# Thirty-two more tokens by gathered rows, one part of the one-hot products on ScalarE, and one block's search in an earlier stage

## The reference, cut to what matters

```
q = (xc @ w_q).reshape(T, 8, 2, 128)
sc = einsum('chpd,hpkd->chpk', q, sub_keys)          # 2 x 128 scores a head
top_s, top_i = top_k(sc, 16)
cand = top_s[:, :, 0, :, None] + top_s[:, :, 1, None, :]
best_s, best_flat = top_k(cand.reshape(T, 8, 256), 16)
expert = ia * 128 + ib                               # 128 experts a token, of 16,384
g = softmax(best_s)
a = gelu(einsum('cd,chkd->chk', xc, u[expert])) * g
out = einsum('chk,chkd->cd', a, v[expert])
```

## Time and profile before

| | |
|---|---|
| median of 3 runs | 1765.27 us (1763.88 to 1772.72) |
| profiled execution, its own time | 1763.86 us |
| its span (first to last instruction) | 1762.0 us, mean granted clock 0.99 |
| PE, PEld, DVE, ACT, POOL busy | 1681.3, 1550.5, 1346.3, 654.0, 401.3 us |
| moved by DMA | 425.82 MB, 242 GB/s over the span |

### The profile page before, as it was taken

One profiled execution on the slowest core, in us unless ns is written; L12 is line 12 of the kernel. 1 busy time (PEld: TensorE's weight loads), 2 busy tenths in 40 slices (PEclk: granted clock), 3 DMA queues, 4 the chain that ended last, 5 costly groups with the idle time before them and its releaser, 6 DMA issues. The chain is left out here.

```text
span 1762.0 us, 26368 instructions
## 1 busy us (share of the span) xinstructions
PE 1681.3 (95%) x9808; PEld 1550.5 (88%) x9808; DVE 1346.3 (76%) x2819; ACT 654.0 (37%) x1027; POOL 401.3 (23%) x282
## 2 busy tenths in 40 slices
PE   5999999999789999999999999999999999999996
PEld 4897766687578999999999999999999999999996
DVE  5433555563566789989989989859988897989898
ACT  5114544441242433443434444433333332333331
POOL 0000000000001021112100112235544554555450
PEclk9999999999899999999999999999999999999998
DMA  5721111022234477778767769999999999999992
GB/s 168 196 89 48 49 48 37 13 86 84 69 93 136 145 276 238 232 251 288 272 252 248 270 213 349 346 385 392 404 366 404 401 396 383 385 390 395 385 402 82
DMA packets 157886, 425.82 MB, mean 242 GB/s; under 512 B 15912, under 2 KB 77520, under 8 KB 155840
## 3 DMA queue, kind: packets, MB, share of 16 engines
q1 hardware_dynamic: 96400, 229.52, 36.8%
q0 software_dynamic: 39472, 144.28, 22.3%
q10 hardware_dynamic: 21888, 50.34, 7.7%
HBM read 365.87 MB, written 58.21 MB: 241 GB/s over the span
## 5 line engine op out<-in xcount | busy, mean ns | idle before, releaser
L431 PE MATMUL psS<-hT_lo,hi 128*128 128x384 f32 (+2 forms) x1504 | 526.6, 350 | 6.6 <-DVE hT_lo L953 5.9
L432 PE MATMUL psS<-hT_hi,lo 128*128 128x384 f32 (+2 forms) x1504 | 518.1, 344 | 0.0
L433 PE MATMUL psS<-hT_hi,hi 128*128 128x384 f32 (+2 forms) x1504 | 515.6, 343 | 0.0
L422 DVE TENSOR_TENSOR lo<-raw,hi 128x1024 fp32r<-128x1024 f32 x323 | 395.0, 1223 | 107.6 <-ACT hi L418 106.2
L418 ACT ACTIVATE hi<-raw 128x1024 fp32r<-128x1024 f32 x323 | 339.0, 1050 | 148.2 <-PE psS L433 111.1
L431 PEld LDWEIGHTS psS<-hT_lo,hi 128*128 128x128 f32 x1504 | 283.5, 188 | 34.8 <-issue 14.8
L541 POOL DMA_INDIRECT gat<-in_u_rows,idx x128 | 185.6, 1450 | 536.0 <-DVE gat L1099 488.4
L433 PEld LDWEIGHTS psS<-hT_hi,hi 128*128 128x128 f32 x1504 | 284.7, 189 | 13.2
L432 PEld LDWEIGHTS psS<-hT_hi,lo 128*128 128x128 f32 x1504 | 284.2, 189 | 10.8
L541 POOL DMA_INDIRECT gat<-in_v_exp,idx x128 | 199.1, 1555 | 197.2 <-DVE y_row L1105 156.5
L708 ACT ACTIVATE act_hi<-act_t 128x384 fp32r<-128x384 f32 x128 | 67.3, 526 | 340.0 <-DVE act_t L1146 340.0
(11 more groups left out here) (278 smaller groups left out, 2540.0 us busy)
## 6 DMA issues: line engine op xcount, KB each, us to landing
raw<-in_u_exp SPq DMA_DIRECT2D x128, 512.0 KB, 4.2
raw<-in_v_exp SPq DMA_DIRECT2D x128, 512.0 KB, 11.3
gelu_dram<-gelu ACTq DMA_DIRECT2D x128, 192.0 KB, 4.0
gel_in<-gelu_dram SPq DMA_DIRECT2D x128, 192.0 KB, 12.1
gates_dram<-gates ACTq DMA_DIRECT2D x12, 1792.0 KB, 9.6
raw<-in_w_merge SPq DMA_DIRECT2D x24, 512.0 KB, 3.4
gate_even<-gates_dram SPq DMA_DIRECT2D x8, 1536.0 KB, 17.2
gate_odd<-gates_dram SPq DMA_DIRECT2D x8, 1536.0 KB, 17.1
```

Source lines behind the costliest of these rows:

```text
L422: nc.vector.tensor_tensor(lo[:, n % RING, :], raw[:, n % RING, :], hi[:, n % RING, :].bitcast(F32), ALU.subtract).then_inc(lo_done, 1)
L431: nc.tensor.matmul(out_ap, w_h, x_l, start=start, stop=False)
L432: nc.tensor.matmul(out_ap, w_l, x_h, start=False, stop=False)
L433: return nc.tensor.matmul(out_ap, w_h, x_h, start=False, stop=stop)
```

## The change

Four edits.

1. The last 32 tokens (EXTRA) leave the dense part: DENSE becomes 352. They are gathered too, with four partitions for each token, each with 32 of its 128 experts (MORE = 32 more columns of DOT and AXPY, 320 items in place of 256). ScalarE repeats each of these tokens' columns four times (y_more), TensorE turns them (8 matmuls behind slab 0), their indices and weights go through memory (idx_dram, g_dram) to the new layout, and 8 matmuls with a matrix of ones (C_SUM) add the four partitions at the end. Batches of gates fall from 48 to 44, the chunks stored from 12 to 11. GATHERS falls from 8 to 6, because of memory.
2. hotG_lo moves to ScalarE, as 8 activations of 128 x 128 a batch (`hot_low_parts`). TensorE takes a batch two steps after `hot`, no longer one.
3. The search of the second block stands in the query stage beside that of the first (six of its heads before the U stage), and each block's decode comes earlier. best, topi and flat get a second buffer for it.
4. The planner has new costs and no fill at the end: it raises the share of TensorE's time that VectorE may use (from 0.98 in steps of 0.005) until all 320 items fit. By its table 59 items stand in steps 0 to 88 (37 before), 71 in steps 89 to 124 (32 before), and 190 from step 125 on (187 before), the last in step 249 (251 before).

```diff
-DENSE = SEQ - P
+EXTRA = 32
+PARTS = P // EXTRA
+DENSE = SEQ - P - EXTRA
-GATHERS = 8
+GATHERS = 6
+MORE = SLOTS // PARTS
+COLUMNS = SLOTS + MORE
-BATCH_AT = [31 + 2 * b for b in range(16)] + [67 + 2 * b for b in range(16)] + [100 + b for b in range(16)]
+BATCH_AT = [19 + 2 * b for b in range(16)] + [55 + 2 * b for b in range(16)] + [91 + 2 * b for b in range(12)]
+SEARCHES = sorted([(FIRST_PQ + 4 + 2 * h, FIRST_PQ + 5 + 2 * h, 0, h) for h in range(HEADS)] +
+                  [(FIRST_PQ + 5 + 2 * h + 7 * (h // 6), FIRST_PQ + 6 + 2 * h + 7 * (h // 6), 1, h) for h in range(HEADS)] +
+                  [(FIRST_U + 14 + 4 * h, FIRST_U + 16 + 4 * h, 2, h) for h in range(HEADS)] +
+                  [(FIRST_U + 48 + 4 * h, FIRST_U + 50 + 4 * h, 3, h) for h in range(HEADS)])
...
-    tensor = [4.15] * (2 * NKEYS)
+    tensor = [3.81] * (2 * NKEYS)
...
+    share = 0.98
+    while True:
+        counts, room = [0] * (2 * NKEYS), 0.0
+        for s in range(9, 2 * NKEYS - 4):
+            room += share * tensor[s] - vector[s]
+            while room > 0 and counts[s] < 2 and sum(counts) < len(ITEMS):
+                counts[s] += 1
+                room -= 1.22 if ITEMS[sum(counts) - 1][0] == DOT else 1.29
+            room = min(room, 1.2)
+        if sum(counts) == len(ITEMS):
+            return counts
+        share += 0.005
...
                 nc.scalar.activation(h_row[:, :], wide[2], ACT.Copy)
+                nc.scalar.activation(h_more, wide[3].rearrange("p (k d) -> p k d", k=KT), ACT.Copy)
...
+            def hot_low_parts(b):
+
+                r, at = b % 2, b * CHUNK % P
+                act.wait_ge(hotB_done, b + 1)
+                for c in range(CHUNK):
+                    last = nc.scalar.activation(hotG_lo[:, r, c // 2, :, c % 2], hotB[:, r, c // 2, :, c % 2], ACT.Copy,
+                                                scale=gT_lo[:, at + c:at + c + 1])
+                last.then_inc(hot_lo_done, 1)
+
+            def store_last_block():
+
+                act.wait_ge(g_done, NBLK - 1)
+                act.dma_start(idx_dram, idx_last[P - EXTRA:P, :]).then_inc(more_out, 16)
+                act.dma_start(g_dram, best[P - EXTRA:P, (NBLK - 1) % 2, :]).then_inc(more_out, 16)
...
+                if s in BATCH_AT:
+                    hot_low_parts(BATCH_AT.index(s))
+                if s - 2 in BATCH_AT:
                     evacuate_batch(evacuated_batches)
...
-                own.mark(V.tensor_tensor(hotG_hi[:, r], hotB[:, r], spread(gT_hi), ALU.mult))
-                V.tensor_tensor(hotG_lo[:, r], hotB[:, r], spread(gT_lo), ALU.mult).then_inc(hot_done, 1)
+                V.tensor_tensor(hotG_hi[:, r], hotB[:, r], spread(gT_hi), ALU.mult).then_inc(hot_done, 1)
...
+                if j == SLOTS:
+                    V.tensor_scalar(y_more[:, :], row, coef[:, j:j + 1], None, ALU.mult).then_inc(item_done, 1)
+                    return
+                total = y_row if j < SLOTS else y_more
...
             def dense(k):
-                return hT_hi[:, k, P:SEQ]
+                return hT_hi[:, k, P:P + DENSE]
...
+                        last = mm(banks[bank][:, DENSE:SEQ - P], y_more[:, m * P:(m + 1) * P],
+                                  cst[:, C_SUM:C_SUM + EXTRA], start=True, stop=True)
```

More of the change, by code:

```diff
@@ L94, in items_per_step @@
             vector[at + part] += cost
-    tensor = [4.15] * (2 * NKEYS)
+    tensor = [3.81] * (2 * NKEYS)
     for at in BATCH_AT:
-        vector[at] += 2.6
-        tensor[at + 1] += 0.95
+        vector[at] += 1.95
+        tensor[at + 2] += 0.95
     for s in range(NKEYS - AHEAD, 2 * NKEYS - AHEAD):
-        vector[s] += 1.06
+        vector[s] += 0.98
     for at in TURN[1:]:
         vector[at + 1] += 0.7
-    counts, room = [0] * (2 * NKEYS), 0.0
-    for s in range(9, 2 * NKEYS - 4):
-        room += 0.98 * tensor[s] - vector[s]
-        most = 1 + s % 2 if BATCH_AT[-1] < s < NKEYS else 2
-        while room > 0 and counts[s] < most and sum(counts) < len(ITEMS):
-            counts[s] += 1
-            room -= 1.22 if sum(counts) <= 3 * SLOTS // 4 else 1.29
-        room = min(room, 1.2)
-    last = 2 * NKEYS - 5
-    while sum(counts) < len(ITEMS):
-        counts[last] += 1
-        last -= 1
-    return counts
+    share = 0.98
[10 more added lines that the diff above has]
+        share += 0.005
 AHEAD = 3
@@ L393, in build, with staging @@
         block = ctx.enter_context(nc.Block())
+        def staging(q):
+            return (q + STORES) % 2
+        stores_of = [sum(staging(q) == r for q in range(STORES)) for r in range(2)]
         def slab_source(n):
@@ L1473, in turn_keys @@
                 turn(banks[4][:, P:2 * P], keys[:, 1, :], ident)
[L1474 removed]
+                turn(banks[5][:, 0:P], best[:, t % 2, :], ident).then_inc(idx_turned, 1)
             pe.wait_ge(sc_done, N_PQ)
@@ L1485, in _ @@
                     for k in range(KT):
-                        last = turn(wide[2][:, k * P:(k + 1) * P], acc[:, k, 0:P], ident)
+                        turn(wide[2][:, k * P:(k + 1) * P], acc[:, k, 0:P], ident)
+                    for k in range(KT):
+                        if k == 0:
+                            pe.wait_ge(repeated, 1)
+                        last = mm(wide[3][:, k * P:(k + 1) * P], y_more[:, k * P:(k + 1) * P], ident, start=True, stop=True)
                     last.then_inc(row_turned, 1)
```

191 lines of the change are left out of this document (118 added, 73 removed).

## The result

The changed kernel takes 1777.12 us in the median of 8 runs (1772.25 to 1785.23), the kernel before 1764.58 (8 runs, 1761.76 to 1774.88). The ratio is 1.0066, with a 95% interval of 1.0036 to 1.0096: 0.7% slower. The forecast was 1722, with a range of 1696 to 1752. It missed the range and the sign.

What follows compares the result with a forecast made beforehand. TensorE, with VectorE about equally loaded, was to set the pace until about step 89, then DMA transfers: 598 + 1 + 1 + 379 + 697 + 3 + 40 = 1719, or 1722 us after execution and profiling corrections; range 1696 to 1752.

Steps and rivals of the forecast that it cites:

- I take 1 us, range 0 to 4: Query stage: VectorE's 7.1 us a position against TensorE's 6.9 drifts 2 us over 11 positions; 1 us added.
- three slabs ahead in lo: Query stage: VectorE works three slabs ahead in lo, a reason to take 1 us for the drift of 2.
- Two engines at the same load never interlock perfectly; I add 2: 379: U stage, steps 0 to 88: VectorE's 374 us and TensorE's 377 fit together, with 2 us added for interlock.
- VectorE's 374: Steps 0 to 88: lo 101, batches 62, search parts 109, items 68, four decodes 34 us.
- ScalarE or VectorE sets the U stage: Rival, chance 0.06: narrow margins cost 0.25 to 0.5 us a step over 89 steps, 22 to 45; total 1744 to 1767.
- its sign: Forecast wrong if VectorE or ScalarE is busy without a gap in steps 19 to 80 and TensorE waits.
- I take 397: From about step 89, transfers set the pace: 276.7 MB at 397 GB/s, 697 us; bounds 385 (719) and 412 (672).
- near 4.15: V stage: steps expected near 4.15 us in the changed profile, where TensorE's own pace was put at 3.82.
- The turn: Between U and V stages: 3 us added, as the 697 us of transfers already hold most of today's turn.
- The ring: Six gather buffers: 12.1 us loop, 526 us, hidden under 697; slower-case rival, chance 0.05: landing 14.5 gives 1825.
- The columns: TensorE matmuls: 352 columns start 159 ns apart, 13.9 ns less each, 86 us over 256 slabs.
- The tail: End of the kernel: 40 us, being 41 less 5 x 0.33, plus 1.

Runs made afterwards that it cites:

- The product put back: Changed kernel with hotG_lo back on VectorE, all else and the plan as changed: 1801.2 us, ratio 1.0211.
- the limited version: Changed kernel with at most one item a step in steps 114 to 129 (two before), as many items in all: 1776.5 us, ratio 1.0053.
- e6: Changed kernel with 384 columns and 256 items again, keeping moved search, hotG_lo on ScalarE and ring of six, own plan: 1793.1 us, ratio 1.0185.
- e10: Kernel before, with its ring of eight, and only hotG_lo moved to ScalarE: 1763.8 us, ratio 0.9981.

## Why the prediction was wrong

Its numbers cut at its own borders, forecast against the profiled run: gelu 0 at 602.9 against 613.8; gelu 0 to 88 376 against 398.9; from there to the last lo 712 (697 + 3, and the 12 us of the earlier trace rows between 1721 and the last lo) against 735.8; the tail 28 against 33.1. That is 10.9 + 22.9 + 23.8 + 5.1 = 62.7 us over the forecast span.

**"I take 1 us, range 0 to 4" (query stage)** failed by size. Measured 7.6 by the search put back. VectorE's position is 7.31 us long, as the starts of pq_lo show, where 7.1 was worked out, against 6.9 of TensorE; the 0.4 a position adds up (4.5 us over 11 positions, where 2 were worked out and 1 was taken), and at the end the slabs of U can't begin, because TensorE's queue has the last scores first. VectorE, then ScalarE, which waited 6.50 us for the last score product:

```profile
588.52 0.68 DVE L1201 TENSOR_TENSOR pq_lo<-psS,pq_hi 128x512 fp32r<-128x512 f32 x1
...
595.83 0.69 DVE L1201 TENSOR_TENSOR pq_lo<-psS,pq_hi 128x512 fp32r<-128x512 f32 x1
...
603.14 0.68 DVE L1201 TENSOR_TENSOR pq_lo<-psS,pq_hi 128x512 fp32r<-128x512 f32 x1
```

```profile
599.65 0.60 ACT L685 ACTIVATE sc<-psO 128x512 f32<-128x512 f32 x1 [0.69 <-PE psO L459]
606.75 0.60 ACT L685 ACTIVATE sc<-psO 128x512 f32<-128x512 f32 x1 [6.50 <-PE psO L459]
```

Being "three slabs ahead in lo" doesn't help: pq_lo, which the scores need, stands behind the search at its own position. The other 4.7 us of the 10.9 are t0.

**"Two engines at the same load never interlock perfectly; I add 2: 379"** is the step whose mechanism failed. TensorE's prices under it held: where it isn't held up the steps are 3.84 and 4.83 (steps 23 to 34), and hotG_lo costs 0.31 on ScalarE. But TensorE stood for 17.7 us and ran at 0.97 of its clock, so gelu 88 came 399 us behind gelu 0 and not 376.

One term of VectorE's 374 was too small. The four decodes were put at 34 us, as what was left of a sum of busy times, while the searches were priced from start to start, with the short gaps inside them. One decode takes 10.5 us in the trace of the changed kernel (steps 13 to 16), so four are an estimated 42, and the sum is 382: more than TensorE's 377, and not less. The waits shown above agree: in these 399 us VectorE waited for others for 17.4 (13.5 of them for ScalarE's hi), so its own work with its gaps filled 381.5. The busy share doesn't tell this. It is 371 of 399 us, 93%, and in the kernel before 366 of 400, where TensorE had no gap.

The work comes in lumps too (a decode of 10.5 us in four steps of 3.84, searches of 5.35). The product put back (20 us of VectorE, 13.3 longer) and the small effect of ScalarE's load (43 us, 4.2 shorter) show that it was mainly VectorE's load. Where the 17.4 us of waits come from wasn't taken apart further. The rival *ScalarE or VectorE sets the U stage* named this, with 0.06 and 22 to 45 us, and its sign was in the list of what would prove the forecast wrong; the chance was far too low. A sum of 374 beside one of 377 should have been read as a warning and not as a fit. From step 65 on the gelus of batch steps stand 7.5 and 1.3 us apart in turn, 8.8 a pair where two steps of TensorE are 8.67: ScalarE then waits for hotB ahead of the gelu, as the prediction feared, at little cost.

**"I take 397" (DMA rate)** was mis-sized. From step 89 to the last lo the changed kernel moved 387 GB/s in 732 us, and the 276.7 MB at 387 are 18 us more than at 397. For the V stage the mechanism was right and is now shown: it falls to TensorE's pace when the bytes are halved and not when VectorE's work is. For steps 89 to 124 it is shown in part: half the bytes make them 8.5 us shorter, half the AXPY work 5.3, one buffer less 7.8 longer. "The range of demand is what changes, not the mixture of transfers" gave one rate for two stages that don't share one: the same kernel moved 404 GB/s in steps 89 to 124 and 382 in the V stage. The V steps were forecast "near 4.15" and are 4.30. The kernel before moved 384 from gelu 127 to its last lo, and that was the number to take for the V stage; the 392 of the earlier trace rows is that of a window that begins 8 us and ends 12 us earlier, and 412 was one window of 10 us.

The Trainium skill (DMA: Bandwidth & Descriptors, Where 436 GB/s comes from) has a memory limit of about 358 GB/s a core. The changed kernel, which runs on one core, contradicts it as well: 387 over 732 us.

**The turn, "+ 3"**: it took 11.5 us more than before. How much of that is a wait of its own and how much is bytes, the limited version leaves open. With half the bytes in the AXPY gathers it took 23.6 us, 6.4 less.

**The ring** behaved as forecast in V (VectorE waits 0.7 us), and not in steps 89 to 124, where gathers land in 10.4 us (17.4 at most) and VectorE waits 23.2 us for them. The prediction had one mean loop for both. **The columns**: 160 ns for 159. So the slope decided rightly over the weight loads' busy share, and the rule of the Trainium skill (Perfetto Trace Analysis, Identifying the Most-Contended Engine), to judge by the weight loads' busy share, was rightly left aside: the weight loads are busy for 476 of 480 us in the half-row kernel at a pace of 3.84.

**The tail** is 4 us longer than before. It isn't mainly the eight small matmuls: the kernels without them, e6 and e10, have 33.9 and 33.7 us as well. From its statistics of the last products of TensorE (from 1765.62 us on, before from 1746.19) the final norm takes 16.0 us to the end, as before (15.8). What grew is the way from VectorE's last lo to it, 17.1 us against 13.3 (e10: 17.9): TensorE had more left to do when VectorE made its last lo.

Put together: each of the 64 added items moves 0.524 MB, at 387 GB/s 1.35 us, in all 87 us; the columns save TensorE 86. In a stage that already stood at its transfer rate the trade could return nothing. What was left to win, the first 89 steps, needed VectorE to have room, and the change filled it.

The trade alone didn't make the kernel slower, though. Beside e6_dense384, which has only the other two edits, the changed kernel is 16 us faster in the median and 8.3 by the stages: 12.9 us are won in steps 0 to 89, and from there to the last lo it is 5.8 longer. Beside the kernel before, e6 is 28.5 us slower in the median and 23 by the stages. So what made it slower than before came mainly with the moved search, its schedule, its plan and the ring of six; of these only the query stage's part, 7.6 us, is separated by a run.

## What to carry to other kernels

Before work is moved from a compute engine to rows fetched by index, price the trade in the resource that the moved work uses: here bytes at the stage's own mean rate, not the best window's. When two engines come out within 2% of each other in a sum, don't forecast the larger sum; look at how large the lumps are, and allow for more (here, in this one case, the stage took 6% more than the larger sum). Price every term of such a sum the same way, from start to start: a rest of busy times leaves out the gaps. A test that keeps every instruction and halves the bytes, with its counterpart that keeps the bytes and halves the arithmetic, tells a transfer bound from an engine bound in two runs.
